# Small experts as tasks of 64 slots with high and low token parts side by side in the stationary operand

## The reference

```python
def moe_swiglu(h, w_router, w_gate, w_up, w_down):
    b, l, d = h.shape
    t = h.reshape(b * l, d)
    logits = jnp.matmul(t, w_router).astype(jnp.float32)
    top_val, top_idx = lax.top_k(logits, TOP_K)  # 2 of 8
    gates = jax.nn.softmax(top_val, axis=-1)
    combine = jnp.sum(jax.nn.one_hot(top_idx, N_EXPERTS, dtype=jnp.float32) * gates[..., None], axis=1)
    out = jnp.zeros((b * l, d), jnp.float32)
    for e in range(N_EXPERTS):
        y_e = swiglu(t, w_gate[e], w_up[e], w_down[e])    # 3584 hidden columns
        out = out + combine[:, e:e + 1] * y_e
```

## Time and profile before

| | us |
|---|---|
| median of 3 runs | 1828.62 |
| lowest, highest | 1828.38, 1829.67 |
| the profiled execution | 1828.04 |
| its span | 1826.4 |

### The profile page before, as it was taken

How to read it: one execution, slowest core, us unless ns; L and a number is a source line. 1 busy time by engine, 2 the same in 40 slices (tenths; PEclk the granted TensorE clock), 3 DMA queues, 4 the chain that set the end, 5 groups by cost and what they waited for, 6 DMA issues and landing times.

```text
span 1826.4 us, 26398 instructions
## 1 busy us (share of the span) xinstructions
PE 1807.2 (99%) x9194; PEld 1532.2 (84%) x9194; DVE 1513.1 (83%) x1858; ACT 1262.7 (69%) x1660; POOL 138.7 (8%) x230
## 2 busy tenths in 40 slices
PE   9999999999999999999999999999999999999998
PEld 7888888888888899888888888888888888888876
DVE  6686787778666688585999999999999999999997
ACT  6645565556544666666787778787787877777776
POOL 2040050000000000140230000000000000000100
PEclk9999999999999999999999999999999999999999
DMA  9423568554554555514999999999999999999994
GB/s 336 154 94 139 177 189 337 198 193 139 192 196 167 178 169 185 184 47 161 340 377 397 389 366 405 375 366 400 371 387 373 379 390 380 379 381 370 406 375 185
DMA packets 176163, 512.57 MB, mean 281 GB/s; under 512 B 11036, under 2 KB 58490, under 8 KB 161674
## 3 DMA queue, kind: packets, MB, share of 16 engines
q1 hardware_dynamic: 172146, 493.08, 72.8%
q0 software_dynamic: 3808, 18.38, 2.5%
q10 hardware_dynamic: 144, 0.26, 0.0%
HBM read 505.38 MB, written 12.07 MB: 283 GB/s over the span
## 4 chain that ended last, share of the span: by engine, by line
PE 92%; DVE 5%; ACT 1%; issue 1%; DMA 0%; POOL 0%; SPq 0%; DVEq 0%; ACTq 0%; POOLq 0%
PE ps L264 24%; PE ps L266 24%; PE ps L265 24%; PE ps L2601 9%; PE ps L2604 4%; DVE w_lo L257 2%; PE ps L2890 1%; PE ps L2396 1%; PE ps L2759 1%; DVE arena L2140 0%; DMA raw<-in_w_in_dram 0%; ACT w_hi L248 0%; PE ps L2854 0%; PE ps L2319 0%; PE ps L2340 0%
## 5 line engine op out<-in xcount | busy, mean ns | idle before, releaser
L257 DVE TENSOR_TENSOR w_lo<-raw,w_hi 128x1024 fp32r<-128x1024 f32 x937 | 1098.7, 1227 | 115.8 <-ACT w_hi L248 110.3
L248 ACT ACTIVATE w_hi<-raw 128x1024 fp32r<-128x1024 f32 x938 | 939.6, 1057 | 258.1 <-PE ps L266 247.6
L264 PE MATMUL ps<-w_hi,a 128*128 128x512 f32 (+1 forms) x1216 | 478.7, 394 | 2.8 <-DVE w_lo L257 1.1
L266 PE MATMUL ps<-w_hi,a 128*128 128x512 f32 (+1 forms) x1216 | 472.3, 388 | 0.0
L265 PE MATMUL ps<-w_lo,a 128*128 128x512 f32 (+1 forms) x1216 | 471.9, 388 | 0.0
L264 PE MATMUL ps<-w_hi,a_hi 128*128 128x512 f32 (+1 forms) x720 | 280.6, 390 | 1.7 <-DVE w_lo L257 1.5
L266 PE MATMUL ps<-w_hi,a_lo 128*128 128x512 f32 (+1 forms) x720 | 278.7, 387 | 0.0
L265 PE MATMUL ps<-w_lo,a_hi 128*128 128x512 f32 (+1 forms) x720 | 278.6, 387 | 0.0
L264 PEld LDWEIGHTS ps<-w_hi,a 128*128 128x128 f32 x1216 | 228.4, 188 | 52.2 <-DVE w_lo L257 3.3
L266 PEld LDWEIGHTS ps<-w_hi,a 128*128 128x128 f32 x1216 | 228.3, 188 | 47.5
L265 PEld LDWEIGHTS ps<-w_lo,a 128*128 128x128 f32 x1216 | 228.6, 188 | 44.8
(11 more groups left out here) (398 smaller groups left out, 1454.0 us busy)
## 6 DMA issues: line engine op xcount, KB each, us to landing
raw<-in_moe_w_gate_dram SPq DMA_DIRECT2D x112, 1024.0 KB, 7.0
raw<-in_moe_w_up_dram SPq DMA_DIRECT2D x112, 1024.0 KB, 7.3
raw<-in_moe_w_down_dram SPq DMA_DIRECT2D x112, 1024.0 KB, 7.2
raw<-in_ssd_w_in_dram SPq DMA_DIRECT2D x24, 1024.0 KB, 5.0
raw<-in_w_ffn_in_dram SPq DMA_DIRECT2D x22, 1024.0 KB, 5.0
raw<-in_w_in_dram SPq DMA_DIRECT2D x21, 1024.0 KB, 6.5
raw<-in_w_ffn_out_dram SPq DMA_DIRECT2D x11, 1024.0 KB, 4.8
raw<-in_dense_w_gate_dram SPq DMA_DIRECT2D x11, 1024.0 KB, 5.1
```

Of the source, the lines that this page charges most:

```text
L248: nc.scalar.activation(w_hi[:, u % SPL, part], raw[:, u % RAW, part], ACT.Copy).then_inc(hi_done, 1)
L257: last = nc.vector.tensor_tensor(w_lo[:, u % SPL, part], raw[:, u % RAW, part], w_hi[:, u % SPL, part].bitcast(F32), ALU.subtract)
L264: nc.tensor.matmul(o, lh, rh, start=start, stop=False, skip_group_check=True)
L266: return nc.tensor.matmul(o, ll, rh, start=False, stop=stop, skip_group_check=True)
```

## The change

An expert with up to 64 tokens runs as a small task. Its stationary operand holds the high parts of 64 tokens in columns 0 to 63 and their low parts in columns 64 to 127. Multiplied by `w_hi` and by `w_lo` (`mm2`), that is two products in place of three; the result has the contribution of the high parts in rows 0 to 63 and of the low parts in rows 64 to 127 (the fourth, low by low, is in it too). Rows r and r + 64 must then be added before the silu. ACT copies gate and up results out of PSUM (`gate_out`, `up_out`), PE adds the two halves and transposes in one product with `m_fold`, two identities of 64 stacked on each other (`fold`), and silu, product, high and low part follow on the folded data, in pieces of 512 and 256 elements (`small_silu`, `small_product`, `small_hi`, `small_lo`). The down product gives again two halves, which ACT and DVE scale and add.

Weights are split by whole units (`whole=True`) in small tasks, one instruction of 2048 elements in place of two of 1024.

Which experts are large is decided by rank: expert 0 and the two others with the most tokens run at 128 slots, expert 0 first, the two others last; all others run in between in tasks of 64 slots, as many as they need. `tables`, `slots` and a new `task_table` compute this on DVE. In the first task PE, ACT and DVE otherwise do what they did. SP's loads per task are the same and in the same order.

```diff
+        def mm2(o, l, rh, rl, start, stop):
+
+            nc.tensor.matmul(o, l, rh, start=start, stop=False, skip_group_check=True)
+            return nc.tensor.matmul(o, l, rl, start=False, stop=stop, skip_group_check=True)
...
-        def split_hi(act, u, rounds=0, halves=(0, 1)):
+        def split_hi(act, u, rounds=0, halves=(0, 1), whole=False):
...
+            if whole:
+                nc.scalar.activation(w_hi[:, u % SPL, :], raw[:, u % RAW, :], ACT.Copy).then_inc(hi_done, 2)
+                return
...
+                def gate_out(i, h):
...
+                    nc.scalar.activation(m_sg[:, h % 2, :].rearrange("p (b r q) -> p b q r", b=2, r=2),
+                                         ps[GATE_BANK[h]][:, :].rearrange("p (b q r) -> p b q r", b=2, r=2),
+                                         ACT.Copy).then_inc(m_silu, 1)
...
+                def small_silu(i, j):
+
+                    n = S * len(STEP_H[j])
+                    act.wait_ge(m_tr, HALVES * i + STEP_H[j][-1] + 1)
+                    nc.scalar.activation(m_st[:, 0:n], ps[0][:, 0:n], ACT.Silu).then_inc(m_ssilu, 1)
...
+                def small_step(i, before, j):
+
+                    gate_u, up_u, down_u = WIDE[j]
+                    if j == 0:
+                        up_out(i, 0)
+                    whole_hi(i, gate_u + 2, gate_u + 3, up_u, up_u + 1)
+                    gate_out(i, 2 * j + 1)
+                    gate_out(i, 2 * j + 2)
+                    whole_hi(i, up_u + 2)
+                    small_silu(i, j)
+                    whole_hi(i, up_u + 3, up_u + 4)
+                    small_hi(i, before, j)
+                    whole_hi(i, up_u + 5)
+                    up_out(i, 2 * j + 1)
+                    up_out(i, 2 * j + 2)
...
+                def small_step_lo(i, before, j):
+
+                    gate_u, up_u, down_u = WIDE[j]
+                    whole_lo(i, gate_u + 2, gate_u + 3, up_u, up_u + 1, up_u + 2)
+                    small_product(before, j)
+                    whole_lo(i, up_u + 3, up_u + 4)
+                    small_lo(i, j)
+                    whole_lo(i, up_u + 5)
...
+                def fold(i, j):
+
+                    pe.wait_ge(m_mult, HALVES * i + STEP_H[j][-1] + 1)
+                    for n, src in enumerate((m_sg, m_act)):
+                        for k, h in enumerate(STEP_H[j]):
+                            for c in range(4):
+                                at = k * S + c * HALF
+                                last = nc.tensor.matmul(ps[n][:, at:at + HALF], src[:, h % 2, c * P:(c + 1) * P], m_fold,
+                                                        start=True, stop=True, skip_group_check=True)
+                    last.then_inc(m_tr, len(STEP_H[j]))
...
                 tables()
-                slots()
                 first_step_lo(0, True)
-                wide_step_lo(0, 0)
+                wide_step_lo(0, 0, slots)
                 positions()
-                wide_step_lo(0, 1)
+                wide_step_lo(0, 1, task_table)
...
-                with pe.Fori(0, n_last) as i:
-                    task(i, True)
-                    project(0, ps[2], 7 * i + 7, i + 1)
-                    project(2, ps[6], 7 * i + 7)
+                with pe.Fori(1, n_small) as i:
+                    small_task(i)
+                    small_units(0, (2,), 7 * i + 7, 4, i + 1)
+                    small_units(2, (6,), 7 * i + 7, 4)
                     pe.wait_ge(m_yhi, 2 * i + 2)
```

More of the change, by code:

```diff
@@ L43 @@
 NE, FE = 8, 3584
-MAX_TASKS = NE + (2 * S - NE) // P
+HALF = 64
+MAX_TASKS = 16
+N_BEFORE, N_LAST, N_TASKS = 16, 19, 20
 UC = 2048
@@ L1352, in silu @@
                         act.wait_ge(unit_used, used(M0 + WIDE[h // 2][0] + 3, 7 * i))
-                    if not start or h > 1:
+                    if h == 0 and not start:
+                        act.wait_ge(m_tr, HALVES * i)
+                    elif not start or h > 1:
                         act.wait_ge(m_mult, HALVES * i + h - 1)
@@ L2008, in _ @@
                 gate = [slot_src[:, 0:T, 1], slot_src[:, T:2 * T, 1]]
-                nb, end, start = R[15][:, 0:NE], R[16][:, 0:NE], R[17][:, 0:NE]
                 first_e = R[18][:, NE:2 * NE]
+                order, large, rest, parts, end, place, base, swap = (m_tab[:, NE * k:NE * (k + 1)] for k in range(8))
+                over, key = m_tab[:, 64:128].rearrange("p (e f) -> p e f", e=NE), m_tab[:, 128:136]
+                step, over4 = m_tab[:, 136:140], m_tab[:, 160:192].rearrange("p (e k) -> p e k", k=4)
+                rho, whole, left, back = (m_tab[:, 192 + 16 * k:208 + 16 * k] for k in range(4))
+                over3 = m_tab[:, 256:304].rearrange("p (n k) -> p n k", k=3)
+                below, same = (m_tab[0:1, 320 + 128 * k:448 + 128 * k].rearrange("p (i e) -> p i e", e=NE) for k in range(2))
+                small_e, large_e = m_tab[0:1, 576:592], m_tab[0:1, 592:608]
                 e21 = m_rt[:, 20, 0:T]
@@ new lines, in tables @@
+                    C.link(nc.vector.tensor_tensor(over4, bcast(rest, 2, 4), bcast(step, 1, NE), ALU.is_gt))
+                    C.link(nc.vector.tensor_reduce(parts, over4, AX.X, ALU.add))
+                    C.link(nc.vector.tensor_tensor_scan(end, ones[:, 0:NE], parts, 0.0, ALU.mult, ALU.add))
+                    C.link(nc.vector.scalar_tensor_tensor(rho.rearrange("p (t e) -> p t e", t=T), bcast(large, 1, T), -float(P),
+                                                          ps[5][:, 0:T * NE].rearrange("p (t e) -> p t e", t=T),
+                                                          ALU.mult, ALU.add))
```

303 lines of the change are left out of this document (248 added, 55 removed).

## The result

| | before | after |
|---|---|---|
| median of the runs (us) | 1828.5 | 1858.33 |
| ratio, with its 95% interval | | 1.0162 (1.0150 to 1.0174) |
| span of the profiled execution | 1826.4 | 1856.5 |
| first result rows leave at | 986.89 | 999.82 |
| one small task, mean of five (before: a middle task) | 118.3 | 122.2 |

A forecast was written before the change was run, and what follows sets the result against it. PE bounds the kernel before, loads the small tasks (107.2 us at 422 GB/s). Five tasks x (118.33 - 107.2) = -55.7, tables +3.5: span 1774.2, plus 2.2 gives 1776.4 us; range 1757 to 1810.

The forecast's parts named there:

- PE's sum: PE in a small task: products 76.2, folds 7.0, transposes of token rows 1.0, sum 84.2 us, 34 less than before.
- New waits: Waits of silu, product, high and low parts in small tasks: hidden behind splits, costed at nothing beyond the engines' own time.
- That slack of 4 us is why lateness costs nothing: Six load buffers go round in 15.3 us, 11.2 of it used; the 4 us left absorb lateness inside a step.
- rival A: Lateness adds up through three split slots: 110 to 116 us a small task, say 113; 1805.6 us in all; chance 0.15.
- DVE, ACT: Engine time in a small task: DVE 100.1 to 103.6 us, ACT 95 to 101, both under the loads.
- The loads: Weight loads of a small task don't shrink: 45.1 MB at 422 GB/s, 107.2 us, and become the bound.
- Rivals B and C: B: queue not full, 395 GB/s, 114.1 us a task, chance 0.07. C: loads bind already, 1832 us, chance 0.03.
- F: Loads do better, 433 GB/s or above: 104.1 us a small task, 1757.5 us in all; chance 0.04.
- SP's and POOL's queues keep their order and their bytes: Transfers queued by SP and POOL: a small task still writes and reads rows of 128 slots; no cost was added.
- The tables: DVE's routing in task 0: 18 more small operations at 0.19 us, 3.4 in all; 3.5 us taken.
- rival D: PE loses its clock in small tasks: at half clock 160 us a task, +209, 2038 us in all; chance 0.05.
- E: An expert passes 64 tokens, so a ninth task costs 107 us: 1883 us in all; chance 0.02.

The follow-up runs named there:

- that run: The changed kernel with both splits in small tasks touching only 512 of 2048 columns, result wrong by it: ratio 0.9755, 1783.0 us against the kernel before.

## Why the prediction was wrong, by its steps

**PE's sum: the fold was mis-sized.** It was put at 56 x 0.125 = 7.0 us a task and is 13.0; a block of 16 at 2.0 and is 3.7. The row it came from stood there: 88 rows of 128x64 in plain f32 at 0.125 each. But these are not 88 products. The program has 4 products in each of 16 steps at that line, 64, and the trace has 88 + 40 = 128 rows of it (40 under another name, since one of three buffers lies elsewhere). So a product of two plain f32 operands leaves two rows, as the fold does (112 rows for 56 products), and 0.125 is the time of a row, not of a product. Counting the products in the program against the rows would have told it. The kernel before, then one small task:

```profile
L2759 PE MATMUL ps<-arena,gla 128*128 128x64 f32 x40 | 5.0, 268 | 0.0
```
```profile
L3196 PE MATMUL ps<-arena x112: 217/275/275, 1140.3 to 1223.1; 128*128 128x64 f32 x112
```

**New waits: this is the step that failed.** The text went through silu, product and the two parts and took the gate copies to stand ahead of the folds. They wait themselves, on `m_tr` in `gate_out`, for the fold of the pieces before. So the cover named for the silu (a copy and a split in front of it) wasn't there: what waits first is the copy, 38.2 us in twelve waits, and the next split is queued behind it. Earlier folds took 4.3 us off a task, shorter ones 7.0. At the last fold of a task, where no copy stands ahead, the silu itself waits in spite of its split: 9.6 us in four waits, up to 2.6.

**"That slack of 4 us is why lateness costs nothing": wrong slack.** Six buffers let the loads run ahead, and the working of that slack may be right. But lateness is paid at the three slots of split units, a circle in which ACT waits for PE, PE for DVE and DVE for ACT. This was rival A, and its evidence is all there: ACT waits for PE's slots (42.1 us in four tasks) and hardly for loads, which run at 378. Its price, 113 us a task, was too low. With the fold early and the copies plain the task does take 113.4; that the two agree so well is partly luck, since A's one half was a guess. The other 8 us go with the two terms that A counted at half or not at all, and with what the clock lost by them. Halves against whole units (2.2 and 2.3 us) and folds in parts (2.2 us) confirm the circle from two further sides.

**DVE, ACT: right.** 100.0 and 97.0 us, whole splits at 2.285 and 1.916 (2.286 and 1.910 in the earlier trace rows):

```profile
L261 DVE TENSOR_TENSOR w_lo<-raw,w_hi 128x2048 fp32r<-128x2048 f32 x168 | 376.1, 2285 | 82.3 <-ACT w_hi L249 82.1
L249 ACT ACTIVATE w_hi<-raw 128x2048 fp32r<-128x2048 f32 x167 | 315.1, 1916 | 44.1 <-PE ps L281 42.1 <-DMA raw<-in_moe_w_up_dram 1.8
```

But engine time being right, what follows from it was not: a sum below the bound was taken as free, and 7.5 us of strided writes in ACT cost 6.0.

**The loads: right as a floor.** 105 to 109 us at 419 to 422 GB/s once nothing else holds the circle. Rivals B and C fell with that run, and F (104.1) is not reached either. As for the Trainium skill ("DMA: Bandwidth & Descriptors", section "Where 436 GB/s comes from"), the 358 GB/s per core that it names for HBM to SBUF were passed again, now by whole tasks at 422. The same page (section "Measured (HBM→SBUF, 128 partitions, SWDGE, issued from GpSimd)") gives that number for two cores that share a memory; here one core runs.

**"SP's and POOL's queues keep their order and their bytes": wrong.** The table of result rows has 16 tasks' rows instead of 11, 14.70 MB are written instead of 12.07, and the stage starts 7.0 us later. The limit of tasks is one changed constant, and the fill that depends on it runs hundreds of us before everything else that was changed.

**The tables: mis-sized.** Forecast 3.5, measured 5.9 to the first result rows. DVE's operations of `slots` in task 0, first and last of 12, and PE's product behind them:

```profile
908.49 0.17 DVE L2231 TENSOR_TENSOR arena<-arena 128x8 f32<-128x8 f32 x1
...
910.91 0.17 DVE L2243 TENSOR_TENSOR arena<-arena 128x16 f32<-128x16 f32 x1
```
```profile
913.63 0.47 PE L274 MATMUL ps<-w_hi,a 128*128 128x512 f32 x1 [2.70 <-DVE w_lo L267]
```

2.6 us of DVE there and 2.0 for the task table (941.90 to 943.99, not before 933), 4.6 together where 3.8 was worked out for the two, and they were not hidden: PE stands 2.70 us behind the first and 2.68 behind the second, where the kernel before has 0.7 us of such waits in task 0. After the first of them PE's clock falls as well, and ten products take 3.65 us from start to start instead of 2.27:

```profile
916.00:919.00 3.00, 3.00 (x11) 2.40 (x10) 2.86 (x9) 0.70 (x1) 0.46 (x1) 0.68 1.01 403
```

From the first expert load to the first result rows PE is idle for 5.6 of 179.8 us, in the kernel before for 1.0 of 174.0, and it is busy 1.2 us longer. That is nearly the whole of the 5.9. It is the same error as with the folds: a block on one engine was held to be covered and was passed on in full.

What makes the surplus of the first small task, 3.9 us over the others, wasn't isolated. The four register loads stand at its start, on ACT and on PE:

```profile
L1540 ACTq TENSOR_LOAD <-tasks x4: 273/276/490, 998.4 to 1000.2; - x4
...
L3276 PEldq TENSOR_LOAD <-tasks x4: 295/306/497, 1007.5 to 1009.6; - x4
```

The first and the last of four start 1.8 and 2.1 us apart, on engines that the prediction held to have slack. They may be half of it; this is argued, not shown. Every run but one shows a surplus (3.2 to 5.5 us); with the short splits it is gone (105.0 against 104.9 to 109.0 for the others), so it seems to be paid only while the circle sets the pace.

**The clock (rival D): its sign was right, its size was not.** The third and fourth small task have a granted clock of 0.94 against 0.99 in the second, and are 2.5 us longer. Two stretches of the third:

```profile
1266.00:1269.00 3.00, 0.75 (x3) 0.66 (x4) 3.00 (x3) 3.00 (x3) 0.00 (x0) 1.00 1.00 414
1269.00:1272.00 3.00, 3.00 (x9) 2.07 (x9) 3.00 (x2) 1.96 (x3) 0.00 (x0) 0.59 1.01 416
```

PE is busy for 0.75 of 3 us, and in the next three, although always busy, it shows a clock of 0.59, that is near the lower of the two levels. PE's longest wait in such tasks is 2.5 us in the changed kernel; with the fold early, the copies without stride, both, and the folds in parts it is 1.6 to 1.7, and the clock is 1.00, with PE's busy share much the same (85 to 90%, against 84 to 86%). So, as far as these runs show, the lower clock follows from the waits and makes two of the tasks some 2% longer; in the repaired kernels it is gone.

**Large task -2.1 us.** It takes 116.2 to 116.3 in every kernel with small tasks in front of it but the one with short splits (118.4), and 118.3 without small tasks. Why was not tested.

**The chances.** Slower had 0.07, from D and E. Neither happened as told; rival A happened and passed its own upper bound (116), since its terms were counted at half. The range ended at 1810 where the mechanism that was named could carry 1860.

## What to carry to other kernels

Where several engines pass a unit round through a few slots, the time of the circle counts, and work "with slack" on any of them (a block of folds, a strided copy) is paid nearly in full; spread it in pieces between the units, and keep units small enough that the next engine can start on a half. For each instruction moved or added read every wait of its function, the one that guards the buffer it writes too, and compare the count of its kind in the program with the count in the trace before a row's price is taken for it. A changed constant has to be followed to every transfer whose size depends on it, however far away it runs.

## What was not expected of the hardware

A product of plain f32 operands is two rows in the trace: 128x64 takes 0.23 us, where the fast format does 512 columns in 0.227. A transpose of plain f32 data is one row: 28 a task in the program, 168 rows for six tasks, 0.13 us each. An ACT write with a stride takes 1.12 to 1.15 us for 128x512, a contiguous one 0.596. The Trainium skill ("SBUF — State Buffer", section "Door 1: The DMA port swizzle (why `[64,N]` ≈ `[32,N]`)") says that accesses that leave a 16-byte line at each step pay a penalty; the trace agrees, with a factor of 1.9 for these writes.

A conversion of 128 numbers on POOL, one per partition, took 0.19 us in the changed kernel and 8.9 us in the one with folds in parts. For each of the two, POOL's instruction and DVE's run of splits beside it:

```profile
1133.01 0.19 POOL L779 CAST slot_idx<-slot_io 128x1 int32 x1 [7.36 <-DMA result_rows<-arena]
...
1124.27 8.88 DVE L261 TENSOR_TENSOR w_lo<-raw,w_hi 128x2048 fp32r<-128x2048 f32 x4
```
```profile
1113.66 8.92 POOL L780 CAST slot_idx<-slot_io 128x1 int32 x1 [7.99 <-DMA result_rows<-arena]
...
1104.30 18.23 DVE L267 TENSOR_TENSOR w_lo<-raw,w_hi 128x1024 fp32r<-128x1024 f32 x16
```

In both, the conversion ends 0.05 us after DVE's run without a gap does (1133.20 after 1133.15, 1122.58 after 1122.53), and so it is in the next three tasks with folds in parts, where it takes 9.2 to 9.8 us (the first of them 1221.97 to 1231.42, DVE's run ending at 1231.37). So POOL seems to get its turn when DVE pauses, which no run isolated. The Trainium skill ("SBUF — State Buffer", section "SBUF: two separate sides") says that DVE and POOL share a port pair which an instruction of either holds to its end; a DVE instruction with two SBUF inputs does so only against a POOL instruction that reads SBUF, as this conversion does. The trace agrees in kind, and goes further: POOL was kept out over a whole run of DVE instructions, some eight of them, not over one.
